# The two feed-forward norms of a decoder trunk by halves of the tokens, and two more places for weights

## The reference, cut to what matters

```python
for layer in range(DEPTH):                  # DEPTH = 2
    h = rms_norm(x, mix_norm[layer])
    y = retention(h, ...) if layer == 0 else rglru_block(h, ...)   # both end in "@ w_out"
    x = x + y
    gate, up = jnp.split(rms_norm(x, ffn_norm[layer]) @ w_gu[layer], 2, axis=-1)
    x = x + (jax.nn.silu(gate) * up) @ w_down[layer]
return rms_norm(x, final_norm)

def rms_norm(x, gain):
    return x * lax.rsqrt(jnp.mean(x * x, axis=-1, keepdims=True) + NORM_EPS) * gain
```

## Time and profile before

| | |
|---|---|
| median of 3 runs | 2811.53 us |
| profiled execution | 2815.13 us, of which the traced span is 2813.3 us |
| PE busy | 2712.8 us (96%) |
| DVE, ACT, POOL busy | 1344.8, 826.1, 1266.7 us |
| mean granted TensorE clock | 0.985 |

### The profile page before, as it was taken

One profiled execution on the slowest core, in us unless ns is written; L12 is line 12 of the kernel. 1 busy time (PEld: TensorE's weight loads), 2 busy tenths in 40 slices (PEclk: granted clock), 3 DMA queues, 4 the chain that ended last, 5 costly groups with the idle time before them and its releaser, 6 DMA issues.

```text
span 2813.3 us, 35922 instructions
## 1 busy us (share of the span) xinstructions
PE 2712.8 (96%) x12145; PEld 2245.7 (80%) x12145; DVE 1344.8 (48%) x1854; ACT 826.1 (29%) x1398; POOL 1266.7 (45%) x1219
## 2 busy tenths in 40 slices
PE   7999999999998799999999999999987999999997
PEld 6888888888887688888888788787865888888886
DVE  7423423423424564455554636456455454545545
ACT  4220220210124423333323523415354222322223
POOL 3323323323322555665555445354335555655553
PEclk9999999999999899999999999999998999999998
DMA  3102102112111021111211111111110211111211
GB/s 132 42 27 68 40 28 68 42 31 65 45 31 49 19 64 52 52 45 52 62 54 50 36 43 53 36 53 38 38 53 16 68 52 52 45 47 56 61 52 75
DMA packets 173483, 140.06 MB, mean 50 GB/s; under 512 B 8656, under 2 KB 142928, under 8 KB 173392
## 3 DMA queue, kind: packets, MB, share of 16 engines
q1 hardware_dynamic: 171664, 133.53, 15.9%
q10 hardware_dynamic: 1728, 5.26, 0.6%
HBM read 133.51 MB, written 5.24 MB: 49 GB/s over the span
## 4 chain that ended last, share of the span: by engine, by line
PE 91%; DVE 4%; ACT 3%; issue 1%; POOL 1%; DMA 0%; POOLq 0%; SPq 0%; DVEq 0%; ACTq 0%
PE ps L563 30%; PE ps L566 30%; PE ps L567 30%; POOL f_h_lo L509 1%; DVE uc L1650 0%; PE ps L622 0%; DVE h_sum_a L1469 0%; DVE residual L1353 0%; ACT f_h_hi L1077 0%; DVE residual L1563 0%; DVE residual L1724 0%; ACT f_h_hi L1082 0%; PE ps L690 0%; DVE xn L1309 0%; DVE gate_buf L1655 0%
## 5 line engine op out<-in xcount | busy, mean ns | idle before, releaser
L466 POOL TENSOR_TENSOR f_w_lo<-f_raw,f_w_hi 128x512 fp32r<-128x512 f32 x263 | 341.6, 1302 | 403.8 <-ACT f_w_hi L1040 403.7
L563 PE MATMUL ps<-f_h_hi,f_w_hi 128*128 128x512 f32 x1232 | 483.7, 393 | 20.9 <-POOL f_h_lo L509 20.4
L566 PE MATMUL ps<-f_h_lo,f_w_hi 128*128 128x512 f32 x1232 | 482.4, 392 | 0.0
L567 PE MATMUL ps<-f_h_hi,f_w_lo 128*128 128x512 f32 x1232 | 482.2, 391 | 0.0
L435 POOL TENSOR_TENSOR small<-w_raw 128x1 f32<-128x1 f32 x200 | 52.7, 264 | 882.4 <-PE ps L563 867.1
L1563 DVE TENSOR_TENSOR residual<-ps,residual 128x512 f32<-128x512 f32 x352 | 239.1, 691 | 166.5 <-PE ps L567 166.5
L563 PEld LDWEIGHTS ps<-f_h_hi,f_w_hi 128*128 128x128 f32 x1232 | 233.4, 189 | 71.0 <-POOL f_h_lo L509 21.2
L563 PE MATMUL ps<-f_w_hi,f_act_hi 128*128 128x512 f32 x696 | 272.1, 391 | 6.9 <-POOL f_last_lo L466 6.9
L446 POOL TENSOR_TENSOR w_lo<-w_raw,w_hi 128x512 fp32r<-128x512 f32 x200 | 271.1, 1356 | 16.0
L1040 ACT ACTIVATE f_w_hi<-f_raw 128x512 fp32r<-128x512 f32 x263 | 165.1, 628 | 374.8 <-PE ps L567 354.3
L567 PEld LDWEIGHTS ps<-f_h_hi,f_w_lo 128*128 128x128 f32 x1232 | 233.2, 189 | 48.9
(11 more groups left out here) (234 smaller groups left out, 4719.3 us busy)
## 6 DMA issues: line engine op xcount, KB each, us to landing
f_raw<-in_ffn_w_gu SPq DMA_DIRECT2D x176, 256.0 KB, 3.3
w_raw<-in_ret_w_in SPq DMA_DIRECT2D x96, 256.0 KB, 2.8
f_raw<-in_ffn_w_down SPq DMA_DIRECT2D x88, 256.0 KB, 2.8
w_raw<-in_lru_w_in SPq DMA_DIRECT2D x48, 256.0 KB, 2.9
w_raw<-in_ret_w_out SPq DMA_DIRECT2D x32, 256.0 KB, 2.6
w_raw<-in_lru_w_out SPq DMA_DIRECT2D x24, 256.0 KB, 2.7
residual<-in_x SPq DMA_DIRECT2D x8, 512.0 KB, 6.5
out_y<-residual SPq DMA_DIRECT2D x8, 512.0 KB, 2.6
```

The lines of the kernel that those rows point to most:

```text
L466: nc.gpsimd.tensor_tensor(lo, src, hi.bitcast(F32), ALU.subtract).then_inc(f_wready, 1)
L563: m = nc.tensor.matmul(o, l_hi, r_hi, start=start, stop=False, skip_group_check=onto)
L566: nc.tensor.matmul(o, l_hi, r_lo, start=False, stop=False, skip_group_check=onto)
L567: return nc.tensor.matmul(o, l_lo, r_hi, start=False, stop=stop, skip_group_check=onto)
```

## The change

The out projection of the last retention head and of the last LRU group goes over token blocks 0 to 3 with all its weight units first, then over blocks 4 to 7 with the same units (`out_by_halves`). So all units have to be kept: beside the ring there are five more places for the retention and three for the LRU (`ro`, `lo`). The FFN norm is taken in two turns: blocks 0 to 3 are squared, scaled, transposed and formed into Q11 and Q21 while PE multiplies for blocks 4 to 7. The quarters' names follow: what was the second form of the first token half is now H_Q21 (channels 4 to 7 of it), and the products' operands are renamed accordingly. The first chunk starts with the four products that take only Q11 and Q21, for both tiles (`PLACES_FIRST`), with the transposes of the second half among them; then come the other ten. POOL gets a sequence of its own for this chunk (`first_units`); it makes the lower parts of T3 and of two of the four pieces of T2. In the last chunk units 16 and 17 both have places of their own, and ACT rounds them right after unit 15. The load of the last norm's gain moves behind a product of the last chunk, since its buffer moved.

The diff, cut:

```diff
+PLACES = [(u, p) for u in range(2) for p in range(PRODUCTS)]
+PLACES_FIRST = [(0, 0), (1, 0), (0, 4), (1, 4)] + [(u, p) for u in range(2) for p in (1, 2, 3, 5, 6)]
+HT_BANK = (4, 5, 6, 7, 4, 5, 6, 7, 1, 2, 3, 5, 6, 7, 2, 3)
...
# POOL, the last head's out units
+                    if last and j >= HEAD_UNITS - 8 + RING:
+                        pool.wait_ge(psum_full, JB_RET + h * HEAD_JOBS + J_T)
+                        used, place = None, out_unit(j - (HEAD_UNITS - 8), ro)
...
# PE
+            def out_by_halves(n, extra, nk, u0, l_hi, l_lo, ready, meanwhile):
+                for half in range(2):
+                    for nh in range(2):
+                        for k in range(nk):
+                            j = nh * nk + k
+                            if half == 0:
+                                pe.wait_ge(w_ready, u0 + j + 1)
+                            if nh == 0:
+                                ready(half, k)
+                            w_h, w_l = out_unit(j, extra)
+                            for i in range(4):
+                                e = by_halves(n, nh, half * 4 + i)
+                                b = i + (4 * nh if half == 0 else 0)
+                                if k == 0:
+                                    free_bank = e - 8 if half == 0 or nh == 0 else e - 4
+                                    pe.wait_ge(psum_free, free_bank + 1)
+                                c = k * S + (half * 4 + i) * P
+                                m = three(bank(b), l_hi[:, c:c + P], l_lo[:, c:c + P], w_h, w_l,
+                                          k == 0, k == nk - 1, half == 0 and i == 0)
+                                if k == nk - 1:
+                                    m.then_inc(psum_full, 1)
+                            if half:
+                                meanwhile(nh, k)
...
+            def early_transposes(layer, nh, k, nk):
+                if (nh, k) == (0, nk - 2):       # transposes 0 to 3
+                elif (nh, k) == (1, 0):          # transposes 4 to 7
...
# retention: wait of each half; LRU: wait of each half and unit
+                        if k == 0:
+                            pe.wait_ge(psum_free, base + J_T + half * 4 + 4)
+                pe.wait_ge(y_ready, (GROUPS - 1) * 6 + half * GT + k + 1)
...
+            def first_products(layer):
+                seen(("q11", 3), ("Q11l", 3))
+                product(n, 0, 0, AT_FIRST)
+                seen(("q21", 0), ("Q21l", 0))
+                product(n, 1, 0, AT_FIRST)
+                for i in range(8, 12):
+                    transposes(layer, i)
+                product(n, 0, 4, AT_FIRST)
+                for i in range(12, 16):
+                    transposes(layer, i)
+                product(n, 1, 4, AT_FIRST)
+                seen(("T1h", 3), ("T1l", 3))
+                product(n, 0, 1, AT_FIRST)
+                seen(("T3h", 3), ("Q22l", 3), ("T3l", 3))
+                product(n, 0, 2, AT_FIRST)
+                seen(("T2h", 3), ("T2l", 3), ("T2l", 1))
+                product(n, 0, 3, AT_FIRST)
+                seen(("T4h", 3), ("T4l", 3))
+                for p in (5, 6):
+                    product(n, 0, p, AT_FIRST)
+                for p in (1, 2, 3, 5, 6):
+                    product(n, 1, p, AT_FIRST)
...
# ACT, last chunk
+                    if last and layer == 1:
+                        ahead(16)
+                        ahead(17)
                     act_round(n, 1, 0)
                     sigmoid_2(n, 1)
                     act_round(n, 1, 1)
...
# DVE
+                adds(0, 0)
+                adds(0, 1)
+                inverse_root(n, 0, 4, turn_a)
+                for half in range(2):
+                    for s in range(4):
+                        scaled(half, s)
+                adds(1, 0)
+                for k in FOUR:
+                    plain(H_Q11, k, k, "q11")
+                for k in FOUR:
+                    plain(H_Q21, k, 4 + k, "q21")
+                adds(1, 1)
+                inverse_root(n, 4, SB, turn_b)
...
+                for k in FOUR:
+                    seen("Q22h", k)
+                    from_bank(t_b[:, t_cut(k)], 12 + k, t_b[:, t_cut(k)])
+                for k in FOUR:
+                    from_bank(t_a[:, t_cut(k)], 12 + k, t_a[:, t_cut(k)])
+                for k in FOUR:
+                    plain(H_Q22, k, 12 + k, "Q22h")
+                for k in (2, 3):
+                    lower(H_T2, k, t_a, "T2h")
...
# SP
-            sp.wait_ge(psum_free, JB_LRU_END)
+            sp.wait_ge(f_mm, chunk_no(1, CHUNKS - 1) * F_MM + AT[1, 0] + 1)
             sp.dma_start(fn[:], ...)
```

More of the change, by code:

```diff
@@ L551, in _ @@
                 units(6, u0 + 12, [n + 4 for n in now])
[L552 removed]
+            units(6, UB_LRU + GROUPS * 18 - 6, [n + GROUPS * 6 - 2 for n in landed], last=True)
             ffn(1)
@@ L646, in norm_and_tile, with head @@
                         products(k - 2)
-            def head(h, first):
+            def head(h, first, last=False):
                 base, ub = JB_RET + h * HEAD_JOBS, h * HEAD_UNITS
@@ L707, in product @@
+            def product(n, u, p, at=AT):
+                j, form = at[u, p], H_OF[p]
                 w_h, w_l = f_unit(j)
@@ L1061, in act_round, with root @@
                 nc.scalar.activation(fa_hi[:, at:at + 512], r3((2, 4)[half] + u), ACT.Copy).then_inc(f_rounded, 1)
-            def forms(layer):
-                g0, fulls, dves = C_FFN + layer * 8, 16 * layer, layer * HN_DVE
-                pools = layer * HN_POOL
-                def scaled(half):
-                    for s in range(DVE_BLOCKS, SB):
-                        c = s * D + half * 512
-                        nc.scalar.activation(xn_at(half, s), X[:, c:c + 512], ACT.Copy,
-                                             scale=rstd[:, s:s + 1]).then_inc(xn_act, 1)
+            def root(n, first, end, turn):
+                act.wait_ge(n_var, turn)
+                nc.scalar.activation(rstd[:, first:end], ssq[:, first:end],
+                                     ACT.Sqrt, bias=eps, scale=1.0 / D).then_inc(n_root, 1)
@@ new lines, in ffn_norm @@
+                for s in range(4, SB):
+                    added(act, n, 1, s)
+                    square_rows(s, 1, r3(s - 4))
+                root(n, 4, SB, turn_b)
+                act.wait_ge(n_rstd, turn_b)
+                for half in range(2):
+                    for s in (6, 7):
+                        at = s * D + half * 512
+                        nc.scalar.activation(xn_at(half, s), X[:, at:at + 512], ACT.Copy,
+                                             scale=rstd[:, s:s + 1]).then_inc(hx_act, 1)
@@ L1148, in chunk @@
                     behind()
-                    for j in (16, 17, 18, 19):
+                    for j in (18, 19) if last and layer == 1 else (16, 17, 18, 19):
                         ahead(j)
@@ L1353, in add, with head @@
                 TT(X[:, c], bank(le), X[:, c], ALU.add).then_inc(psum_free, 1)
-            with dve.Fori(0, HEADS) as h:
+            def head(h, last=False):
                 base = JB_RET + h * HEAD_JOBS
-                step.loop(h, 2)
                 dve.wait_ge(rope_in, h * 32 + 32)
@@ L1472, in lower, with adds, seen @@
-                def lower(form, k, src, at):
-                    dve.wait_ge(hn_act, acts + at + 1)
+                    TS(xn_at(half, s), X[:, c:c + 512], rstd[:, s:s + 1], None, ALU.mult).then_inc(hx_dve, 1)
+                def adds(half, nh):
+                    for i in range(4):
+                        e = by_halves(n, nh, half * 4 + i)
+                        add(e, i + (4 * nh if half == 0 else 0), half * 4 + i, nh)
+                def seen(*what):
+                    dve.wait_ge(hn_act, hn_at(HN_ACT, *what, layer))
@@ new lines, in norm_by_halves @@
+                adds(1, 0)
+                for k in FOUR:
+                    plain(H_Q11, k, k, "q11")
+                for k in FOUR:
+                    plain(H_Q21, k, 4 + k, "q21")
+                adds(1, 1)
+                inverse_root(n, 4, SB, turn_b)
+                for half in range(2):
+                    for s in (4, 5):
+                        scaled(half, s)
+                t_1(0)
+                t_1(1)
+                lower(H_T1, 0, t_a, "T1h")
+                t_1(2)
```

536 lines of the change are left out of this document (335 added, 201 removed).

## The result

| | before | after |
|---|---|---|
| time, median | 2812.27 us (2811.03 to 2813.7) | 2770.48 us (2768.83 to 2771.46) |
| profiled execution | 2815.13 us, span 2813.3 | 2771.12 us, span 2769.2 |

The ratio is 0.985, 95% interval 0.9838 to 0.9862: 42 us less. The forecast of 2756 us was 14.5 us too low. The wide range, 2744 to 2775, holds the time; the forecast's own, 2750 to 2765, does not, and the number lies nearer to the 2774 us of rivals B and D than to the forecast.

A forecast was written before the change was run, and what follows sets the result against it. PE's chain of waits (91%) bounds the kernel. Gains 2 x 22.6 - 1.6 + 3.4 + 8.4 = 55.4 us off 2811.5 give 2756 us (chance 0.62), range 2750 to 2765, with rivals B and C 2744 to 2775.

The forecast's parts named there:

- B: Rival: shared port lets POOL's work hold up DVE nearly every time; junctions gain 15 us each, 2774 us; chance 0.17.
- D: Rival: early weight units come late, 2.3 us for each of five and three units; 18 us lost, 2774 us; chance 0.05.
- The start of the first junction: Out projection's first unit now waits for four lower parts, ending about 854.85, PE free at 853.28: 1.6 us lost.
- The moved transposes: Half the transposes move between out products: 3.9 us, plus 0.2 us waiting for lower parts of Q11, per junction.
- From E to (0,2): From the out projection's end to T3's product: 17.5 us of PE work, then 6.1 us idle, until 23.6 us.
- T4 meanwhile: ... E + 31.0, covered: After T3's product: ten DVE operations, 6.2 us, plus 1.2 us sharing with POOL, finish before T2's product ends at 31.7.
- Later weight units ... are covered, with nothing left over: First chunk's last five products: POOL's 2.5 us per unit fits PE's 2.72 us, after one wait of 0.7 us.
- The start of the second junction: LRU out projection's first half: POOL delays DVE 2.3 us, block 4's bank free at 2065.1; gain 3.4 us, ends 1 and 7.3.
- The last chunk: Last weights: three POOL units at 1.25 us, PE pauses 1.8 us, full pace; gain 8.4 us, 5 if the clock drops.
- The base: Whole kernel: median taken 3.6 us under the profiled execution, so the gain is subtracted from 2811.5 us.
- C: Rival: DVE undisturbed at the second junction, T3 pause without slow clock; gain 64.7 us, 2747 us; chance 0.14.
- E: Rival: clock stays at 1.2 GHz through the junctions, 504 slow products, 101 us more than forecast, 2857 us; chance 0.02.

The follow-up runs named there:

- run with the pause filled: Changed kernel with 24 unused matmuls into a free bank in PE's pause before T3's product, (0,2): median 2770.38 us, against 2770.70 for the changed kernel again.
- run with other banks: Changed kernel with the transposes' banks chosen so that T3's product, (0,2), no longer waits for Q22's lower parts: median 2769.73 us.
- run with unit 8: Changed kernel with ACT rounding the weights of unit 8, for product (0,6), ahead of the load of the sigmoid's table: median 2768.14 us.
- run with undisturbed scans: Changed kernel with POOL preparing the second junction's three later out projection units only behind the last scan: median 2770.65 us.
- run with the wait by halves: Changed kernel with PE, in the last chunk, waiting for each half of the last weights where it uses it: median 2767.80 us.
- last run: Changed kernel with the combined edits except Q22's move and its banks, POOL's late LRU units held, unused matmuls in both first-chunk pauses: median 2755.01 us.
- Q22 late: Changed kernel with other transpose banks and three of Q22's four lower parts made by DVE behind T4's: median 2770.26 us.

## Why the prediction was right in direction and 14.5 us off

**The start of the first junction** (1.6 lost): exact, 1.60 measured.

**The moved transposes** were charged at 3.9 + 0.2 us per junction; the two groups of sixteen took 1.7 us each, 3.3 in all. This hides some 0.8 us per junction of what follows.

**From E to (0,2)**: exact at the first junction, 23.6 us and 6.1 us of pause, and not by luck: ACT's last upper part of Q22 ends at E + 17.4, as summed. At the second it is 24.1, since the four additions there queue behind Q21's last lower part.

**"T4 meanwhile: ... E + 31.0, covered"** is the step that failed first. T4's last lower part ends at 933.96, E + 32.1, as DVE loses 2 us to POOL at T2's lower parts where I had allowed 1.2; and (0,5) does not wait for T4 alone but for DVE's first addition as well, 0.6 us behind, which the sum left out. So (0,5) starts at E + 33.0 (second junction 33.8), not 31.7. The consequence is larger: since T4 binds, the 2.7 us that I charged for the slow products are no price of their own. The run with the pause filled took them away and gained nothing; the run with other banks took them from (0,2) and gained nothing either.

**"Later weight units ... are covered, with nothing left over"** failed next. One unit at 2.5 us of POOL against 2.72 of PE was right where POOL is alone; beside DVE's products of activations its operations take 1.72 to 1.75 us. ACT's order has a part in it too, as the run with unit 8 shows. Forecast 0.7 us of waiting, measured 1.05, 0.38 and 0.39, each with some 0.16 us more between the products' starts. With the step before that is 2.9 of the 3.3 us by which the first junction's products ended late, and 3.7 of the 4.1 at the second.

**The start of the second junction**: block 4's bank came as forecast, and by the mechanism named (the run with undisturbed scans). The banks behind it came later than the 1.88 + 1.2 us taken, as h_lo took 2.36 us for two beside POOL: gain about 1.1 in place of 3.4 us (20.0 for the stretch, less 18.9 of the junction by the measure under the rivals).

**The last chunk**: three units at 1.25 us was wrong beside DVE: the first took 1.30 us, the other two 3.39, and 0.5 us from the end of the last to PE's start were left out. Behind the 3.19 us of pause the clock fell (0.50 from 2738 to 2740). The lower end, "5 if the clock drops all the same", was the outcome: 5.4. The run with the wait by halves gave the missing 3.

**The base**: 3.2 us of the 14.5, from subtracting a gain read off the profiled execution, which was a long one, from the median.

**The rivals.** C, D and E did not come. B named the right mechanism and overstated it: DVE's operations that read a PSUM bank were not held up at all, and the junctions gained 23.4 and 22.3 us behind E, 20.0 and 18.9 with the moved transposes taken off, not 15. That the time came out 3.5 us from B's 2774 is no support for its prices. On the rule that the forecast had weighed (the Trainium skill, SBUF — State Buffer, "SBUF: two separate sides": operations with two SBUF inputs and GpSimd's reads exclude each other for a whole instruction), the trace agrees: 1.1 us more per operation of POOL beside those, none beside L1725's. Its outer bound of 17 us was far off because few of the 14 met POOL: three at the first junction, 3.0 us in all.

**What would have shown me wrong**, by the prediction's last part: T4 later than T2's product, and the chunk behind waiting for POOL. Both happened.

What stays open: why the first junction's end varies from 53.1 to 55.7 us behind the addition of squares in profiles whose code there is the same. In the longer ones the clock fell once more, behind a wait before (0,5) or for a weight; why the waits were longer there was not separated.

## What to carry to other kernels

Behind a long wait look for the one that it hides: to cost a pause, ask what the program would wait for next if it were gone, and add the chains of all engines up to there, with every operation that the next product's semaphores include. Place the helper engine's work beside operations that read PSUM, not beside those with two SBUF inputs: moving it within the latter moves its price without lowering it. Harmless products in a pause gave nothing where another wait stood behind them; whether they pay where TensorE binds behind the pause, the last run suggests and doesn't separate.

## What the runs showed of the hardware

- A pause's length alone did not decide the clock, against the 2 us that I had put down before the last run. The granted clock stayed full behind waits of 1.43, 1.7 and 1.81 us before (0,5), behind one of 2.02 us for a weight (Q22 late, second junction) and behind one of 3.08 us (the filled first pause, first junction). It fell behind 1.77 us for a weight (last weights by halves, first junction), behind 2.03 us (unit 8, first junction: 0.66 in 935 to 940), 2.27 and 3.4 to 3.9 us. The Trainium skill, TensorE: Matmul & The Clock Gate, "Part 1: The HAM clock gate", says that the slow level is the default and activity releases it. The run with both pauses filled, mean clock 0.998 against 0.994, agrees.
- DVE's operations with a PSUM input took 0.66 us each beside POOL and alone, from start to start; with two SBUF inputs 0.60 alone and up to 1.77 us beside it. POOL's own subtractions went from 1.25 to 1.75 us beside those, once to 2.06 (2042.55 in the changed kernel).
